# Prompt attention rewritten by units of 128 queries, with probabilities turned on TensorE two units late

## What is computed

```python
k_nope = einsum('bsr,rhd->bshd', latent, w_uk)       # 8 heads x 64
v      = einsum('bsr,rhd->bshd', latent, w_uv)       # 8 heads x 64
q      = einsum('bsr,rhd->bshd', rms_norm(cq, g_q), w_uq)   # 8 heads x (64 + 32 rotary)
sc = (einsum('bqhd,bkhd->bhqk', qn, k_nope) + einsum('bqhd,bkd->bhqk', qr, k_rope)) * SM_SCALE
sc = where(kpos <= qpos, sc, NEG_INF)
p  = softmax(sc, axis=-1)
o  = einsum('bhqk,bkhd->bqhd', p, v)
```

## Time and profile before

| what | value |
|---|---|
| median of 3 runs | 1981.93 us (1981.62 to 1983.86) |
| the profiled execution, its own time | 1979.38 us |
| its span | 1977.6 us, mean granted clock 0.908 |
| PE busy | 1689.7 us (85%), 13,425 matmuls |
| VectorE, ScalarE, GpSimd busy | 926.0, 547.4, 248.1 us |
| HBM | 92 GB/s over the span |

### The profile page before, as it was taken

How to read it: one execution, slowest core, us unless ns; L and a number is a source line. 1 busy time by engine, 2 the same in 40 slices (tenths; PEclk the granted TensorE clock), 3 DMA queues, 4 the chain that set the end, 5 groups by cost and what they waited for, 6 DMA issues and landing times. The chain is left out here.

```text
span 1977.6 us, 32849 instructions
## 1 busy us (share of the span) xinstructions
PE 1689.7 (85%) x13425; PEld 1480.6 (75%) x13425; DVE 926.0 (47%) x1655; ACT 547.4 (28%) x1027; POOL 248.1 (13%) x230
## 2 busy tenths in 40 slices
PE   5698998377998888887979649999999999999981
PEld 2354544167997667666779649999999999999981
DVE  2577676444234545455424843343333423333337
ACT  0144444322111344443523331211111121112123
POOL 3024353300000201102002320000000000000006
PEclk7799999579999797878889869999999999999995
DMA  9499993411111000000041131212121122112013
GB/s 371 174 354 352 366 368 163 137 41 29 54 43 41 14 14 1 14 0 0 0 139 64 55 118 33 64 32 60 35 64 32 32 64 64 32 32 64 1 54 139
DMA packets 116494, 183.47 MB, mean 93 GB/s; under 512 B 17038, under 2 KB 86358, under 8 KB 112300
## 3 DMA queue, kind: packets, MB, share of 16 engines
q1 hardware_dynamic: 106428, 101.71, 16.3%
q0 software_dynamic: 8192, 75.85, 9.5%
q10 hardware_dynamic: 1776, 4.51, 0.6%
HBM read 172.06 MB, written 9.94 MB: 92 GB/s over the span
## 5 line engine op out<-in xcount | busy, mean ns | idle before, releaser
L1984 PE MATMUL ps<-mix_conv,wf_hl 128*128 128x384 f32 (+1 forms) x1584 | 272.6, 321 | 11.3 <-DVE wf_hl L2009 11.3
L1984 PE MATMUL ps<-mix_attn,wf_hl 128*128 128x384 f32 (+1 forms) x1584 | 271.0, 319 | 0.0
L1984 PEld LDWEIGHTS ps<-mix_conv,wf_hl 128*128 128x128 f32 x1584 | 255.3, 189 | 11.3 <-DVE wf_hl L2009 11.3
L1984 PEld LDWEIGHTS ps<-mix_attn,wf_hl 128*128 128x128 f32 x1584 | 253.7, 188 | 0.0
L1998 PE MATMUL ps<-hid,wd_hl 128*128 128x384 f32 (+1 forms) x1584 | 249.9, 318 | 0.0
L1998 PEld LDWEIGHTS ps<-hid,wd_hl 128*128 128x128 f32 x1584 | 248.8, 188 | 0.0
L2024 DVE TENSOR_TENSOR h<-ps,gate 128x384 f32<-128x384 f32 (+1 forms) x66 | 34.1, 516 | 321.5 <-PE ps L1984 321.5
L2039 DVE TENSOR_TENSOR acc<-ps,acc 128x384 f32<-128x384 f32 (+1 forms) x240 | 123.9, 516 | 93.3 <-PE ps L1998 93.3
L625 DVE STREAM_TRANSPOSE rows_T<-ring 128x1024 f32<-128x1024 f32 x128 | 150.5, 1215 | 29.2 <-DMA ring<-in_cache_latent,idx 26.0
L1653 POOL TENSOR_TENSOR ln_y<-ln_y,ln_g 128x1024 f32<-128x1024 f32 (+3 forms) x18 | 38.2, 2120 | 965.9 <-ACT ln_y L1643 965.7
L1055 PE MATMUL ps<-U,wc_hl 128*128 128x384 f32 (+1 forms) x864 | 138.4, 323 | 8.6 <-DVE wc_hl L1069 8.6
(11 more groups left out here) (324 smaller groups left out, 2460.5 us busy)
## 6 DMA issues: line engine op xcount, KB each, us to landing
ring<-in_w_ada SPq DMA_DIRECT2D x12, 2048.0 KB, 11.4
wf_raw<-in_w_gate SPq DMA_DIRECT2D x22, 512.0 KB, 4.1
wf_raw<-in_w_up SPq DMA_DIRECT2D x22, 512.0 KB, 5.4
wd_raw<-in_w_down SPq DMA_DIRECT2D x22, 512.0 KB, 5.9
wc_raw<-in_w_in SPq DMA_DIRECT2D x24, 256.0 KB, 3.2
x_nat<-in_x_prompt SPq DMA_DIRECT2D x4, 1024.0 KB, 7.5
wo_raw<-in_w_o SPq DMA_DIRECT2D x8, 512.0 KB, 4.1
ln_x<-in_x_prompt SPq DMA_DIRECT2D x8, 512.0 KB, 4.3
```

What stands on the lines that cost most here:

```text
L1984: last = pe.matmul(ps[:, 2 * (q % 2) + g, 0:tn], a, x, start=j == 0, stop=j == 3 * KD - 1)
```

## The change

The stage is rewritten with the same inputs and outputs. Heads go one by one, without a hardware loop: 64 units n, each one block of 128 queries of head n // 8, in the order of query blocks `QB = (6, 7, 4, 5, 2, 3, 0, 1)`. The scores are made once, in three passes, with queries on the partitions; `q` and `k` are projected so that the scores come out negated and scaled, VectorE takes their minimum (`least`), ScalarE the exponential of a whole unit with the minimum as bias and the sum of the row beside it (`exp`). TensorE turns the probabilities of unit n - 2 by 128x128 transposes (`turn`), four to a bank of two banks, ahead of score(n); ScalarE copies the high part out of PSUM (`hi`), VectorE subtracts the rest (`lo`). At every odd step `weigh` takes two units: high and low values stand side by side as 128 stationary columns, so that two passes (high and low probabilities) of up to 256 columns do; the lower 64 partitions of the output are copied (`low`) and added (`out`), and the inverse sums are spread by one float32 matmul per unit. The projections are cut in items: q in two halves per head (steps 8g and, for the next head, 8g + 4), k and v of a pair of heads at steps 2, 3, 6 and 7 of the head before it. The estimates, the row of maxima, `sums` and the 65th column go.

```diff
...
+        QT = sb("QT", [HD, 2, SEQ], F32R)
+        KT = sb("KT", [HD, 2, SLOT3, SEQ], F32R)
+        V = sb("V", [P, SLOT3, NT, P], F32R)
+        prob = sb("prob", [P, 2, SEQ])
+        PT = [sb("PT_even", [P, 2, 8, 2 * P], F32R), sb("PT_odd", [P, 2, 6, 2 * P], F32R)]
+        uq2 = sb("uq_hl", [P, 2, KQ, P], F32R)
...
+        top, sums = sb("top", [P, 4]), sb("sums", [P, NU])
+        o_low, o_sum = trig[0:VD, 0:2 * P], trig[0:VD, 2 * P:4 * P]
+        o32 = sb("o32", [P, 2 * P])
...
+        QB = (6, 7, 4, 5, 2, 3, 0, 1)
+        TURN, OUT, PROJ = 4, 6, 7
+        ITEMS_AT = {-1: [("k", 0, 0, 4), ("k", 0, 1, 5), ("q", 0, 1, 6)]}
...
+        for g in range(H):
+            place(8 * g, "q", g, 0)
+            if g == 0:
+                place(1, "v", 0, 0)
+                place(2, "v", 0, 1)
+            if g + 1 < H:
+                place(8 * g + 4, "q", g + 1, 1)
+            if g % 2 and g + 1 < H:
+                for p, kind, c in ((2, "k", 0), (3, "k", 1), (6, "v", 0), (7, "v", 1)):
+                    place(8 * g + p, kind, (g + 1) // 2, c)
...
+        UQ_AT.update({8 * j - 5: j for j in range(1, H)})
...
+        KV_AT.update({16 * i - 10: i for i in range(1, H // 2)})
+        BATCHES = [(u, k0, min(4, QB[u % 8] + 1 - k0)) for u in range(NU) for k0 in range(0, QB[u % 8] + 1, 4)]
+        OF_UNIT = [[b for b, x in enumerate(BATCHES) if x[0] == u] for u in range(NU)]
+        STEPS = NU + 6
...
+            return (n - 5) // 2 if n >= 5 and n % 2 and (n - 5) // 2 < NU // 2 else None
...
+                pool.tensor_copy(KT[NOPE:HD, :, 2, :], krT[NOPE:HD].bitcast(F32)).then_inc(const_set, 1)
+                for j in range(2 * H):
+                    c = 1 - j % 2
+                    tok = slice(c * 512, (c + 1) * 512)
+                    pool.wait_ge(r_out, j + 1)
+                    pool.tensor_tensor(r1[NOPE:HD], r1[NOPE:HD], r2[NOPE:HD], ALU.add).then_inc(r_sum, 1)
+                    pool.wait_ge(r_hi, j + 1)
+                    pool.tensor_tensor(QT[NOPE:HD, 1, tok], r1[NOPE:HD], QT[NOPE:HD, 0, tok].bitcast(F32),
+                                       ALU.subtract).then_inc(r_lo, 1)
...
+                def exp(u):
+                    n = (QB[u % 8] + 1) * P
+                    act.wait_ge(top_out, u + 1)
+                    if u >= 2:
+                        act.wait_ge(turned, OF_UNIT[u - 2][-1] + 1)
+                    act.activation(prob[:, u % 2, 0:n], flat[:, 1024 * (u % 2):1024 * (u % 2) + n], ACT.Exp, bias=top[:, u % 4:u % 4 + 1],
+                                   scale=-1.0, accum_out=sums[:, u:u + 1]).then_inc(exp_out, 1)
+                def hi(u):
+                    for b in OF_UNIT[u]:
+                        k0, n = BATCHES[b][1:]
+                        act.wait_ge(turned, b + 1)
+                        wait(act, weighed, u // 2 - 1)
+                        act.activation(PT[u // 2 % 2][:, 0, k0:k0 + n, u % 2 * P:u % 2 * P + P],
+                                       ps[:, TURN + b % 2, 0:n * P].rearrange("p (k q) -> p k q", q=P), ACT.Copy).then_inc(pt_hi, 1)
+                def low(k):
+                    act.wait_ge(weighed, k + 1)
+                    wait(act, o_summed, k)
+                    act.activation(o_low, ps[VD:P, OUT, 0:2 * P], ACT.Copy).then_inc(low_out, 1)
...
+                for n in range(STEPS):
+                    if out_at(n - 1) is not None:
+                        low(out_at(n - 1))
+                    if 2 <= n < NU + 2:
+                        hi(n - 2)
+                    if n < NU:
+                        exp(n)
+                    for item in ITEMS_AT.get(n - 1, []):
+                        if n and item[0] == "q":
+                            rotary_hi(item)
+                    for item in ITEMS_AT.get(n, []):
+                        item_hi(item)
+                    if out_at(n - 2) is not None:
...
+                def project(item):
+                    kind, i, c, bank = item
+                    if bank in last_in:
+                        was = last_in[bank]
+                        if was[0] == "q":
+                            pe.wait_ge(q_lo, count(was))
+                            pe.wait_ge(r_out, count(was))
+                        else:
+                            pe.wait_ge(k_lo if was[0] == "k" else v_lo, count(was))
...
+                def score(u):
+                    g, qb = u // 8, QB[u % 8]
+                    if u >= 2:
+                        pe.wait_ge(exp_out, u - 1)
+                    if u % 4 == 0:
+                        pe.wait_ge(q_lo, 2 * g + 1 + u % 8 // 4)
+                        pe.wait_ge(r_lo, 2 * g + 1 + u % 8 // 4)
+                        pe.wait_ge(k_lo, 2 * (g // 2) + 2)
+                    for c in range(qb // 4 + 1):
+                        n = min(512, (qb + 1) * P - c * 512)
+                        diagonal = c == qb // 4
+                        for j, (q, k) in enumerate(split_passes([QT[:, hl, qb * P:(qb + 1) * P] for hl in range(2)],
+                                                                [KT[:, hl, g % SLOT3, c * 512:c * 512 + n] for hl in range(2)])):
+                            last = pe.matmul(ps[:, 2 * (u % 2) + c, 0:n], q, k, start=j == 0, stop=j == 2 and not diagonal)
                         if diagonal:
+                            last = pe.matmul(ps[:, 2 * (u % 2) + c, n - P:n], ident_r[:], mask_r[:], start=False, stop=True)
+                    last.then_inc(scored, 1)
+                def turn(u):
+                    pe.wait_ge(exp_out, u + 1)
+                    for b in OF_UNIT[u]:
+                        k0, n = BATCHES[b][1:]
+                        wait(pe, pt_lo, b - 1)
+                        for j in range(n):
+                            last = pe.transpose(ps[:, TURN + b % 2, j * P:(j + 1) * P],
+                                                prob[:, u % 2, (k0 + j) * P:(k0 + j + 1) * P], ident[:])
+                        last.then_inc(turned, 1)
+                def weigh(k):
+                    g, blocks = k // 4, QB[(2 * k + 1) % 8] + 1
+                    pe.wait_ge(pt_lo, OF_UNIT[2 * k + 1][-1] + 1)
+                    pe.wait_ge(inv_out, 2 * k + 2)
+                    wait(pe, o_scaled, k)
+                    if k % 8 == 0:
+                        pe.wait_ge(v_lo, 2 * (g // 2) + 2)
+                    for kb in range(blocks):
+                        q0 = P if kb == blocks - 1 else 0
+                        for hl in range(2):
+                            pe.matmul(ps[:, OUT, q0:2 * P], V[:, g % SLOT3, kb, :], PT[k % 2][:, hl, kb, q0:],
+                                      start=kb == 0 and hl == 0, stop=kb == blocks - 1 and hl == 1)
+                    for j in range(2):
+                        u = 2 * k + j
+                        last = pe.matmul(ps[0:VD, OUT, (2 + j) * P:(3 + j) * P], sums[:, u:u + 1].to_broadcast([P, VD]), ident[:],
+                                         start=True, stop=True)
+                    last.then_inc(weighed, 1)
...
+                for n in range(STEPS):
+                    if 2 <= n < NU + 2:
+                        turn(n - 2)
+                    if n < NU:
+                        score(n)
+                    for item in ITEMS_AT.get(n, []):
+                        project(item)
+                    if out_at(n) is not None:
+                        weigh(out_at(n))
...
+                def item_lo(item):
+                    kind, i, c, bank = item
+                    tok = slice(c * 512, (c + 1) * 512)
+                    if kind == "q":
+                        at = QT[0:NOPE, :, tok]
+                        dve.wait_ge(q_hi, count(item))
+                        wait(dve, r_lo, count(item) - 1)
+                        dve.tensor_tensor(r1[NOPE:HD], ps[NOPE:HD, bank, :], trig[NOPE:HD, tok], ALU.mult)
+                        dve.tensor_tensor(r2[NOPE:HD], ps[HD:P, bank, :], trig[HD:P, tok], ALU.mult).then_inc(r_out, 1)
+                        dve.scalar_tensor_tensor(at[:, 1], ps[0:NOPE, bank, :], -SM, at[:, 0].bitcast(F32), ALU.mult, ALU.subtract)\
+                           .then_inc(q_lo, 1)
...
+                def least(u):
+                    n = (QB[u % 8] + 1) * P
+                    dve.wait_ge(scored, u + 1)
+                    dve.tensor_reduce(top[:, u % 4:u % 4 + 1], flat[:, 1024 * (u % 2):1024 * (u % 2) + n], AX_X, ALU.min).then_inc(top_out, 1)
...
+                def lo(u):
+                    for b in OF_UNIT[u]:
+                        k0, n = BATCHES[b][1:]
+                        at = PT[u // 2 % 2][:, :, k0:k0 + n, u % 2 * P:u % 2 * P + P]
+                        dve.wait_ge(pt_hi, b + 1)
+                        dve.tensor_tensor(at[:, 1], ps[:, TURN + b % 2, 0:n * P].rearrange("p (k q) -> p k q", q=P),
+                                          at[:, 0].bitcast(F32), ALU.subtract).then_inc(pt_lo, 1)
+                def out(k):
+                    hh = k // 4 % 2
+                    dve.wait_ge(low_out, k + 1)
```

(81 more changed lines are left out.)

417 lines of the change are left out of this document (151 added, 266 removed).

## The result

The changed kernel takes 1933.64 us (median of 4 runs, 1928.63 to 1941.13), the kernel before beside it on the same chip 1981.78 (1980.48 to 1983.86): 0.9759 of the time, 95% interval 0.9726 to 0.9792, or 48 us less. The profiled execution is the slowest of the four, 1941.13 us, so what follows shows the change at its least.

What follows compares the result with a forecast made beforehand. TensorE was taken to bound the old attention stage, not at its peak. Setup 21, steps 260, unseen waits 10, clock 27 and tail 6 give 324 against 364.5 us, hence 1940; range 1904 to 1970, chance 0.62.

Steps and rivals of the forecast that it cites:

- Setup: Start of the attention stage, weights, first projections and rotary through score(0): 21 us.
- The tail: Behind the last unit, exp, turn, hi, lo, weigh and the output: 6 us.
- step 1: Units with n mod 8 = 1: 1.22 + 0.42 + 0.32 + 1.16 + 0.5 = 3.6 us.
- step 5: Units with n mod 8 = 5: 2.6 us.
- steps 6 and 7: Units with n mod 8 = 6 and 7: 5.0 us, TensorE's list, with a weight split on VectorE in even heads.
- the bank chain: Two banks of turned probabilities: a step lasts at least least(n), lo(n-2), turn(n-1)'s last batch, score(n+1) and 0.5 us.
- step 2: Units with n mod 8 = 2: 0.82 + 1.24 + 0.43 + 1.18 + 0.5 = 4.2 us.
- 3 to 4 falls: TensorE's clock in the stage: each fall 12 us at low clock, costing 8; 27 us in all.
- waits that I do not see: Allowance over the stage's steps: 0.15 us per step, 10 us.
- Hand-overs dearer: Crossings between TensorE, VectorE and ScalarE cost 0.5 to 0.8 us more in 64 steps: 1972 to 1991; chance 0.16.
- TensorE does not bind freely: Denies the rival that TensorE bounds the stage, VectorE's queue ahead and clock holding: 1857 to 1887; chance 0.07.
- rival 1: TensorE's clock stays low because light steps 2, 3 and 6 let it fall: 2019 to 2089; chance 0.15.

Runs made afterwards that it cites:

- experiment 1: Changed kernel with VectorE's `out_lo` one step later, behind `lo` of the next step and ahead of `out`: 1924.21 us, ratio 0.9722.
- experiment 5: Changed kernel with one more wait, keeping GpSimd's second rotary operation back until VectorE's `out_lo` of that step is done: 1923.78 us, ratio 0.9707.
- experiment 6: Changed kernel with unused filler matmuls, three of 512 columns, ahead of second transposed batches and in step 6, heads 2, 4, 6, 7: 1933.16 us, ratio 0.9761.
- experiment 7: experiment 1 with VectorE's and ScalarE's part of the q items also one step later: 1910.93 us, ratio 0.9661.
- experiment 2: Changed kernel with `lo` ahead of the minimum in VectorE's list: 1957.06 us, ratio 0.9885.
- experiment 3: Changed kernel with score(n) ahead of the transposes of unit n - 2 in TensorE's list: 1932.2 us, ratio 0.9729.
- experiment 8: experiment 7 combined with experiment 3's order, score(n) ahead of turn(n - 2): 1908.52 us, ratio 0.9633.
- experiment 4: Changed kernel with transposes, `hi` and `lo` one unit back instead of two: 1977.53 us in one run.
- experiment 9: experiment 7 with head 0's first q item left in its place: 1909.69 us, ratio 0.9635.

## Why the prediction held

- **The time.** 1940 predicted, 1933.6 measured; the stage 324 predicted, 322.1 in the profiled execution, which ran 7.5 us above the median. By its total the sum held to 2 us, but its terms less well. If the 7.5 us lie in the stage, the median's stage is nearer 315 (an estimate). The prediction's own sum gives 1938.9 + 2.5 = 1941; 1940 is that rounded down.
- **What bounds it.** TensorE's 32.4 to 26.8 us per head is 45 us for eight heads at full clock; the recorded busy time fell by 298 - 257 = 41. The minimum took 47.7 us (49 predicted).
- **Setup** 20.0 us against 21. The tail, from the last minimum at 948.1 to 961.0, is 13, of which I had counted 6; the steps after the last minimum are real steps. The 297 below holds the last of the 64 steps, the measured 289.3 doesn't.
- **The chain.** Here a term was mis-sized. "3.6" for step 1 and "2.6" for step 5 measured 4.8 and 3.9: the prediction took VectorE's last item as costing 0.42 and left out what it waits for. ScalarE's exponential of the same step stands ahead of `out_hi` (23.5 us in 25 waits), and GpSimd's operation beside it costs up to 0.87 more. Over the eight heads steps 1 and 5 were 17 us longer than forecast. Experiments 1 and 5 took these away, and the steps came to 3.3 and 2.4, and 4.0 and 3.0. The "5.0" for steps 6 and 7 was 6.9 in head 4 (2.1 + 4.8) and more in 2 and 6; that was the clock, since in experiment 6 they took 5.4 in head 4 with no fall in them. Heads 2, 4 and 6 were 35.7, 34.8 and 36.0 instead of 29.2 plus hidden waits of 1.2; heads 1, 3 and 5 were 45.6, 37.5 and 39.1 against 36.2. From the first minimum to the last the steps took 289.3, where the prediction had 297 with waits and clock.
- **Which mechanism.** The prediction had the bank chain as the step's lower bound and VectorE's list beside it. Experiments 1, 5 and 7 show that the list with its waits on ScalarE sets steps 0, 1, 4 and 5. Experiments 2, 3 and 8 show that relieving the bank doesn't shorten the stage: freeing it earlier cost 23 us, passing it by changed nothing in the total, in part because the clock fell more. They also show the bank chain where the prediction had it, in step 2: 4.2 forecast, 4.2 measured at full clock (experiment 1), 2.8 with the bank out of the way (experiment 3). In head 4 steps 0, 3 and 4 (4.8, 3.5, 5.3) fit the 5.1, 3.6 and 5.1; step 2 (5.6) had a low clock in it.
- **The clock.** I predicted 3 to 4 falls, 27 us. In rows of 2 us it fell 14 times, each short, for 77 us at 1.2 GHz. It costs where TensorE is the bound, above all at the end of head 1, whose last step took 10.2 us with TensorE full and at 1.2 GHz (two of its rows; PE busy is the first number behind the length, the clock the third from the end):

```profile
728.00:730.00 2.00, 2.00 (x12) 2.00 (x11) 0.68 (x2) 0.57 (x2) 0.00 (x0) 0.50 0.00 0
730.00:732.00 2.00, 2.00 (x11) 2.00 (x11) 0.00 (x0) 0.00 (x0) 0.00 (x0) 0.50 0.00 0
```

What the falls cost in the steps can be estimated, since a step without a fall hardly differs between heads of one kind (step 0 is 4.8 or 4.9 in heads 1 to 6). Step 7 was 6.2, 4.8 and 6.8 in heads 2, 4 and 6 against 3.3, 3.3 and 3.9 in experiment 6; step 4 was 1.5 or 1.6 longer in heads 0 and 1 than in experiment 1, and in head 5 than in head 3; the last two steps of head 1 took 14.8 against 9.3 in head 3; step 0 of head 7 took 1.3 more than in heads 1 to 6; and step 2 in heads 2, 4, 6 and 7 took 0.7 to 1.3 more than in experiment 1. Together that is 23 us (an estimate, for the slowest of the four runs). So I had far too few falls, each far too dear, and the 27 came out near because the two errors cancel. The 10 us "for waits that I do not see" had no row behind them; the 17 us of steps 1 and 5 were what was not seen. To that extent the sum matched by luck.
- **The rivals.** The low clock did not hold (0.88). Hand-overs dearer by 0.5 us in each step did not come either: steps 1 and 5 had 17 us too much, 0.27 a step over the 64. VectorE itself loses 34 us at `out_lo` (23.5 in waits, and 23.8 - 32 x 0.414 = 10.5 in length), but experiment 1, which takes both away, is only 9 us faster. TensorE does not bind freely. The change does what it says: its two-unit lag is worth 44 us (experiment 4, one run), and the exponential is covered (1.3 us).
- **Transposes.** I counted them as work for the clock on the earlier trace rows. The stage has 288 of them and a clock of 0.88, with 49.2 us recorded busy, 31 us at 0.108 at full clock. The clock falls behind a stop of TensorE, here the 3.14 us wait that ends at 822.34:

```profile
818.00:820.00 2.00, 1.21 (x8) 0.92 (x7) 0.60 (x1) 1.93 (x6) 0.86 (x1) 1.00 0.00 0
820.00:822.00 2.00, 0.00 (x0) 0.00 (x0) 1.97 (x4) 1.14 (x3) 0.40 (x1) 0.80 0.00 0
822.00:824.00 2.00, 1.66 (x9) 1.69 (x9) 1.56 (x5) 1.05 (x3) 0.00 (x0) 0.50 0.00 0
```

The fall to 1.2 GHz comes in the row that has no matmul. The Trainium skill ("TensorE: Matmul & The Clock Gate", Part 4: PE-mode transpose) states that the full clock does not engage for transposes. This stage doesn't bear that out: with transposes among its matmuls it held 0.88, and the low clock of rival 1 did not come. Where they stand alone, in the kernel before, the rows disagree as well.

## What to carry to other kernels

Write down each engine's list for one step and ask of its last item whom it waits for: an item of 0.4 us that waits for another engine's work of the same step holds everything queued behind it, and moving it one step later was worth some 9 us (not clear of noise by itself), with the projections' share of the same list 23. To cover a chain of exponential and subtraction, let the consumer take the work of two units back; one unit back cost 44 us in one run. Compare kernels step by step and with the granted clock beside each step: in experiment 9 a fall cost up to 1.6 us of a step, enough to hide what an edit won in the total. And the sum of a forecast can be right with terms wrong, so compare its terms.

## What the hardware showed that I had not expected

VectorE's SBUF-to-SBUF operation on 64x256 takes 0.41 us, and 1.28 us when GpSimd's 32x512 operation has just begun. In the rows of step 1, GpSimd runs from 819.14 to 820.39 and VectorE's, started at 819.40, ends at 820.68, that is 0.29 after GpSimd: as if held until then. The second place in head 4 has the same picture:

```profile
837.34 1.27 POOL L1255 TENSOR_TENSOR QT<-rot,QT 32x512 fp32r<-32x512 f32 x1 [1.55 <-ACT QT L1291]
837.60 1.29 DVE L1515 TENSOR_TENSOR mix_attn<-o,mix_attn 64x256 fp32r<-64x256 f32 x1 [0.88 <-ACT mix_attn L1318]
```

Again GpSimd ends at 838.61 and VectorE at 838.89. Of the 32 operations 13 were long in this way. With the operation held back (experiment 5), all 32 took 0.41 to 0.42. Operations that read PSUM, such as the minimum of 1.20 us beside GpSimd's L1253 at 815.34 (to 816.60), kept their time. The Trainium skill ("SBUF — State Buffer", Who interferes with whom) states that a VectorE instruction with two SBUF inputs and a GpSimd instruction that reads SBUF contend, that the lock on the ports they share is exclusive, and that the order of issue decides which of them is blocked. The trace agrees: at 819.40 GpSimd still had 0.99 us to run, and VectorE's operation was 0.87 us longer than the usual 0.41. The prediction had priced GpSimd as hidden and missed this.
